# Counters in place of drains, a new order within a slot, and a later first gather in the paged decode of a decoder layer

## Chip, cores and metric

The kernel runs on one core of a Trainium2 chip. The metric is the device time of one execution in microseconds; a run's figure is the median of several executions. The profile is one further execution, recorded instruction by instruction.

## What is computed

One layer of an autoregressive trunk, for one prompt of 1024 tokens and for 8 samples with 8 new tokens each, all in float32. An RMS norm and a wide projection feed three branches: sparse attention (compressed, selected and windowed), a gated convolution and a recurrence. They are joined and projected back. The part that the change touches is the attention of the samples over their cached pages and window:

```python
def _nsa_decode(q, k_c, v_c, k_s, v_s, k_w, v_w, pool_ck, pool_cv, pool_sk, pool_sv, win_k, win_v, page_table, w_ck, w_cv, rel_bias):
    ...
    o_c, p_c = _nsa_compressed(q, q_pos, kc, vc, rel_bias)
    ...
    top_i, valid = _select_blocks(p_c, q_pos, n_sel)
    ...
    ks = jnp.where(is_past, pool_sk[phys[..., None], rows, g5], jnp.pad(k_s, pad)[b5, new_rows, g5])
    vs = jnp.where(is_past, pool_sv[phys[..., None], rows, g5], jnp.pad(v_s, pad)[b5, new_rows, g5])
    key_pos = top_i[..., None] * SEL_BLOCK + s_ar
    o_s = _sel_attend(q, q_pos, ks, vs, key_pos, valid, rel_bias)
    ...
    o_w = _window_dense(q, q_pos, kw, vw, k_pos, rel_bias)
    return o_c, o_s, o_w, _last_rows(kw, w_buf), _last_rows(vw, w_buf)
```

The kernel doesn't gather the selected blocks alone: it loads all cached keys and values of a sample, computes all scores and adds a mask.

## The kernel before

The kernel is one hand-ordered program for each engine, joined by counting semaphores. Its stages: projections with the convolution and the recurrence beside them (to about 500 us), the attention of the prompt tile by tile (`pe_pairs`, to about 671 us), the decode (`pe_decode`, to about 802 us), and the output projection (to the end). TensorE (PE) does matmuls and transposes, VectorE (DVE) and ScalarE (ACT) read PSUM, GpSimd (POOL) issues the indirect gathers and does the last sums of the prompt's attention, SyncE (SP) issues plain loads.

**Decode rounds.** The 8 samples are done in 4 pairs. A round works on two pairs at once: keys and scores of pair `r`, and probabilities and values of pair `p = r - 1`; so there are five rounds (rnd 0 to 4), the first with keys alone, the last with values alone. The cached tokens of a pair are 8 chunks of 512 (c = 0 to 7) and a ninth, the window (`NC` = 8). A round has five slots, `SLOTS = [(0, 1), (2, 3), (4, 5), (6, 7), (NC,)]`. In slot d PE does, in this order:

1. `turn(p, 2d)` and `turn(p, 2d + 1)` (L2025): transposes of the probabilities into the PSUM banks `TURNED`;
2. `pe_decode_keys_turn(pe, r2, chunks[0])` and then `chunks[1]` (L1983): transposes of the keys of the next slot's chunks, 8 for a chunk, into the two banks `KEYS`; both chunks use the same two banks, so the second waits until the first is copied out;
3. `scores(r, mine)` (L2012) of this slot's chunks, into the banks `SCORED`;
4. `values(p, c)` (L2048) of both chunks; in slot 0 `blocks(p)` (L2037), in slot 4 `new_values` (L2061) around the window's values.

**Who copies.** ACT copies turned keys (L1836) and the even turned probabilities (L1824), and does the exponentials `exp` (L1845). An odd chunk is "swapped": one half of its keys is copied by ACT and the other by DVE, in `keys` (L1942, one copy of 64 x 1024). DVE also copies the odd probabilities (L1824), adds masks and finds maxima of the scores in `peak` (L1887, L1890), and in the first slot of rounds 2 to 4 joins the result of the pair before the last (`finish`, L1914 to L1926). DVE's order in a slot: odd probabilities, `finish`, odd keys, peaks.

**Buffers and gathers.** A gather (L1743 for keys, L1755 for values) fetches half of the chunks of one sample; two of them, one for each sample of the pair, make a half (h = 0 for chunks 0 to 3, 1 for chunks 4 to 7), 2 x 1 MB. There is one buffer of keys, so the keys of pair 1 can only be gathered when PE has turned those of pair 0. Before, PE tells this by `pe.drain().then_inc(...)` on four counters: `kused` and `wkused` for keys and window keys (L1986, L1988), `vused` and `wvused` for values (L2052, L2054), and a fifth, `o_d` (L2065), tells DVE that the result of a pair is whole. That is 7 drains in a full round. The last transposes or matmuls of each chunk also count on `kt_ps` or `dv` themselves.

**Around the start of the decode.** `pool_pairs` does the prompt's last joins: for each part a sum (L1577) and, at a tile's end, a product (L1581) that counts on `oz`. At its last part it waits for `kused` and issues the first gathers of pair 1 (`pool_keys(pool, 1, 0)`, L1570) ahead of the last sum. Then `pool_decode` goes on with the second half of the keys, both value halves, and so on in a fixed order. The three last side steps of the prompt's attention (`TAIL_SIDES`: one product with the compressed values, L1595, and two transposes of weights, L1599) are spread over slots 0 to 2 of round 0, each with a DVE step (L1439, L1442). DVE, ACT and POOL may not go on with probabilities before `oz` has reached 8, since the tiles share storage.

**Output.** In round 4 PE fills its gaps with the first products of the output projection (L2171) and then runs it alone.

Of the kernel before, what the change touches and what calls it, by code (L numbers as in the profile page):

```python
# [23 lines left out]
P = 128  # L24
# [8 lines left out]
HD = 64  # L33
# [144 lines left out]
def program(nc, dram, outs, scratch):  # L178
    with ExitStack() as ctx:
# [743 lines left out]
        def carve(a, n):  # L923
# [62 lines left out]
            kt_ps kt_act kt_dve q_swapped dpair kused vused wkused wvused sd_ps sn_ps sd_used mx_sel mx_win ex_d dp_ps o_d o_sb ot_ps   # L986
# [575 lines left out]
        def pool_pairs(pool):  # L1562
            pool.wait_ge(SEM["za_silu"], 2)
            pool_wide(pool, 0)
            for n, m in enumerate(WEIGHTS):
# [3 lines left out]
                if n == len(WEIGHTS) - 1:  # L1569
                    pool.wait_ge(SEM["kused"], 1)  # L1570
                    pool_keys(pool, 1, 0)
# [125 lines left out]

        def after(r, d):

            return (r, SLOTS[d + 1]) if d + 1 < len(SLOTS) else (r + 1, SLOTS[0])  # L1700
# [18 lines left out]
        def keys_bank(b2):  # L1719
            return bank(KEYS + b2)  # L1720
# [52 lines left out]
        def pool_decode(pool):  # L1773
            def keys(pr, h):
                pool.wait_ge(SEM["kused"], 2 * (pr - 1) + h + 1)
                pool_keys(pool, pr, h)

            def values(pr, h):
                before = pr - 1 if h else pr - 2
                if before >= 0:  # L1780
                    pool.wait_ge(SEM["vused"], 2 * before + h + 1)
                pool_values(pool, pr, h)
            keys(1, 1)
            pool.wait_ge(SEM["oz"], NT)
# [11 lines left out]
        def sp_decode(sp):  # L1796
# [6 lines left out]
            for rnd in range(4):  # L1803
                if rnd < 3:
                    sp.wait_ge(SEM["wkused"], rnd + 1)
                    window(rnd + 1, "win_k", kw_d, kw_ld)
                if rnd == 3:

                    for h in range(2):
                        sp.wait_ge(SEM["kused"], 7 + h)  # L1810
                        for k in (2 * h, 4 + 2 * h):
                            sp.dma_start(wo[:, k:k + 2, :], dram["w_out"][:, k:k + 2, :]).then_inc(ld_wo[h], 16)
                if rnd >= 1:
                    sp.wait_ge(SEM["wvused"], rnd)
# [11 lines left out]
        def act_decode(act):  # L1826
            def keys(r, c):
                k = k_no(r, c)
                for b2 in range(2):
# [3 lines left out]
                    o, i = ktc[:, k % 4, b2, :], keys_bank(b2)  # L1833
# [15 lines left out]
            for rnd in range(ROUNDS):  # L1849
                r, p = rnd, rnd - 1  # L1850
                for d in range(len(SLOTS)):
                    if p == 0 and d == 0:
                        act.wait_ge(SEM["oz"], NT)
                    if p >= 0:
                        turned(act, p, 2 * d)
                    r2, chunks = after(r, d)
                    if r2 < 4:
                        keys(r2, chunks[0])
                    if p >= 0 and d < NC // 2:
                        exp(p, 2 + d)  # L1860
                    if r < 4 and d == NC // 2:
                        exp(r, 0)
                        exp(r, 1)
                    if r2 < 4 and len(chunks) > 1:
                        keys(r2, chunks[1])

        def dve_decode(dve):
# [42 lines left out]
            def finish(p):  # L1910
# [9 lines left out]
                dve.wait_ge(SEM["o_d"], p + 1)  # L1920
# [16 lines left out]
            def keys(r, c):  # L1937
# [4 lines left out]
                dve.tensor_copy(ktc[HD:2 * HD, k % 4].rearrange("p b n -> p (b n)"), bank(KEYS, 2)[0:HD]).then_inc(SEM["kt_dve"], 1)  # L1942
# [29 lines left out]
        def pe_decode_keys_turn(pe, r, c):  # L1972
            if c in (0, NC // 2, NC):
                pe.wait_ge(kw_ld if c == NC else kd_ld[c // (NC // 2)], 32 * r + 32)
            k = k_no(r, c)
            for b2 in range(2):
                src = kd[:, b2, c * 512:(c + 1) * 512] if c < NC else kw_d[:, b2, :]
                if k >= 1:
                    pe.wait_ge(SEM["kt_act"], 2 * k - 1 + b2)
                    if b2 == 0:  # L1980
                        pe.wait_ge(SEM["kt_dve"], swapped_to(r, c - 1)) if swapped_to(r, c - 1) else None
                for j in range(4):
                    last = pe.transpose(keys_bank(b2)[:, j * P:(j + 1) * P], src[:, j * P:(j + 1) * P], ident)  # L1983
                last.then_inc(SEM["kt_ps"], 1)
            if c in (NC // 2 - 1, NC - 1):
                pe.drain().then_inc(SEM["kused"], 1)  # L1986
            if c == NC:
                pe.drain().then_inc(SEM["wkused"], 1)  # L1988

        def pe_decode(pe):  # L1990
# [48 lines left out]
            def values(p, c):  # L2039
# [31 lines left out]
            rest = list(TAIL_SIDES)  # L2071
            pe_decode_keys_turn(pe, 0, 1)
            for rnd in range(ROUNDS):
                r, p = rnd, rnd - 1
                for d, mine in enumerate(SLOTS):
                    r2, chunks = after(r, d)
                    if p >= 0:
# [4 lines left out]
                    if r2 < 4:  # L2082
# [435 lines left out]
```

## Time and profile before

| | us |
|---|---|
| median of 3 runs | 924.86 (924.19 to 928.08) |
| the profiled execution | 920.5 |
| its span, first to last instruction | 918.4 |
| PE busy | 866.4 (94%) |
| DVE busy | 621.0 (68%) |
| ACT busy | 369.5 (40%) |
| POOL busy | 121.3 (13%) |
| DMA, over the span | 118.31 MB, mean 129 GB/s |

Busy time is summed for each engine. PE's ends are modelled from the size of an instruction, so successive groups can overlap by some 0.1 us. In the rows below, a time in brackets is the time in which the engine stood idle just ahead of the group, with what ended it; "issue" means that the profile shows nothing that it waited for. L-numbers are lines of the kernel before.

### The profile page before, as it was taken

What the parts mean: (1) busy time and instruction counts of PE and PEld (TensorE: products, weight loads), DVE (VectorE), ACT (ScalarE), POOL (GpSimd) and SP (SyncE); (2) the same over time, 40 slices, a digit from 0 to 9 for tenths busy, and PEclk for the clock granted to TensorE, in tenths of its full rate; (3) what the DMA queues carried; (4) which work ended last, traced back from release to release, by engine and by line L of the source; (5) the groups of instructions that cost most, each with busy time, mean ns of one, the idle gap of its engine ahead of it and who ended that gap; (6) DMA issues with size and microseconds to landing.
All of it is one profiled execution on the core that took longest, in us unless ns stands there. A gap on an engine that the chain in (4) does not pass through costs nothing.

```text
span 918.4 us, 15568 instructions
## 1 busy us (share of the span) xinstructions
PE 866.4 (94%) x5973; PEld 551.1 (60%) x5973; DVE 621.0 (68%) x1149; ACT 369.5 (40%) x878; POOL 121.3 (13%) x129
## 2 busy tenths in 40 slices
PE   6999999999999999999899999998888888999997
PEld 4656665666666666767676776775555655544443
DVE  4688779999888988998466557667875556321222
ACT  4311252310021201025787887776656555410111
POOL 1011210000001011110103222232253220000000
PEclk9999999999999999999999999999999999999999
DMA  8444561422144166440930200000039985522211
GB/s 303 176 138 143 200 206 48 60 53 68 47 137 175 29 223 240 162 161 0 323 166 1 92 3 1 2 1 1 1 109 412 378 336 214 183 94 81 80 61 43
DMA packets 32109, 118.31 MB, mean 129 GB/s; under 512 B 3433, under 2 KB 11771, under 8 KB 22971
## 3 DMA queue, kind: packets, MB, share of 16 engines
q0 software_dynamic: 9360, 68.16, 20.0%
q1 hardware_dynamic: 19053, 43.39, 13.8%
q10 hardware_dynamic: 3623, 5.76, 3.0%
q8 instruction: 48, 0.79, 0.4%
q14 instruction: 25, 0.20, 0.1%
HBM read 108.33 MB, written 13.29 MB: 132 GB/s over the span
## 4 chain that ended last, share of the span: by engine, by line
PE 77%; DVE 10%; ACT 4%; DVEq 3%; issue 3%; DMA 2%; POOL 0%; ACTq 0%; POOLq 0%
PE PS L836 28%; PE PS L2171 12%; PE PS L1616 6%; PE PS L1626 6%; PE PS L1644 5%; PE PS L812 3%; PE PS L1983 3%; DVE main L609 3%; ACT main L1417 2%; PE PS L2025 2%; PE PS L2048 2%; PE PS L2012 2%; DVE main L606 2%; PE PS L1599 1%; DVEq L607 1%
## 5 line engine op out<-in xcount | busy, mean ns | idle before, releaser
L836 PE MATMUL PS<-main 128*128 128x352 f32 (+1 forms) x1056 | 330.1, 472 | 0.0
L836 PEld LDWEIGHTS PS<-main 128*128 128x128 f32 x1056 | 201.3, 191 | 120.7 <-issue 3.6
L1417 ACT ACTIVATE main<-PS,main 128x512 f32<-128x512 f32 (+3 forms) x192 | 103.8, 562 | 50.3 <-DVE main L1457 25.2
L2171 PE MATMUL PS<-main 128*128 128x512 f32 x256 | 111.6, 593 | 0.1
L437 ACT ACTIVATE main<-PS 128x384 f32<-128x384 f32 x24 | 11.8, 490 | 205.5 <-PE PS L836 199.1
L1626 PE MATMUL PS<-cst,main 128*128 128x128 f32 x528 | 73.6, 282 | 15.0 <-ACT main L1417 12.4
L647 DVE SCALAR_TENSOR_TENSOR main<-main,par 128x1022 f32<-128x1022 f32 (+16 forms) x66 | 83.8, 1270 | 5.3 <-issue 0.4
L2171 PEld LDWEIGHTS PS<-main 128*128 128x128 f32 x256 | 47.9, 190 | 58.3 <-issue 58.3
L606 DVE TENSOR_TENSOR main<-main 128x1024 f32<-128x1024 f32 x64 | 75.5, 1220 | 9.6 <-DMA main<-in_cmp_k_dram,row 6.0
L609 DVE TENSOR_TENSOR main<-main 128x1024 f32<-128x1024 f32 (+2 forms) x96 | 75.0, 781 | 7.2
L1626 PEld LDWEIGHTS PS<-cst,main 128*128 128x128 f32 x528 | 57.5, 142 | 30.4 <-ACT main L1417 22.9
L1407 ACT ACTIVATE main<-PS 128x512 f32<-128x512 f32 (+1 forms) x138 | 69.7, 603 | 2.8 <-PE PS L1626 2.4
L1616 PE MATMUL PS<-main 64*128 64x512 f32 (+3 forms) x384 | 68.5, 487 | 0.1
L1644 PE MATMUL PS<-main 128*64 128x128 f32 (+2 forms) x924 | 66.6, 292 | 0.0
L1644 PEld LDWEIGHTS PS<-main 128*64 128x64 f32 x924 | 50.8, 137 | 24.6 <-issue 22.4
L1457 DVE CUSTOM_DVE_ANT_1 PS<-PS,diag 128x512 f32<-128x512 f32 x70 | 46.8, 727 | 16.5 <-PE PS L1616 16.5
L374 POOL DMA_INDIRECT main<-in_cmp_k_dram,row x16 | 19.1, 1192 | 248.7 <-DVE half L611 228.6
L1836 ACT ACTIVATE main<-PS 128x512 f32<-128x512 f32 (+1 forms) x72 | 39.2, 595 | 19.9 <-PE PS L1983 19.5
L2199 ACT ACTIVATE main<-PS 128x512 f32<-128x512 f32 x17 | 10.2, 597 | 89.6 <-PE PS L2171 83.6
L1616 PEld LDWEIGHTS PS<-main 64*128 64x128 f32 x384 | 31.0, 190 | 19.2 <-issue 13.4
L1983 PE MATMUL PS<-cst,main 128*128 128x128 f32 x256 | 35.7, 284 | 7.1 <-ACT main L1836 3.0
L1417 ACT ACTIVATION_READ_ACCUMULATOR main<-PS,main 128x1 f32 x192 | 40.7, 212 | 0.0
(320 smaller groups left out, 1006.5 us busy)
## 6 DMA issues: line engine op xcount, KB each, us to landing
main<-in_w_tiles_dram SPq DMA_DIRECT2D x24, 512.0 KB, 3.7
out_dram<-main SPq DMA_DIRECT2D x18, 256.0 KB, 2.1
main<-in_x_prompt_dram SPq DMA_DIRECT2D x8, 512.0 KB, 9.2
main<-in_w_out_dram SPq DMA_DIRECT2D x4, 1024.0 KB, 7.0
main<-in_x_prompt_dram SPq DMA_DIRECT2D x16, 256.0 KB, 2.9
out_dram<-main SPq DMA_DIRECT2D x4, 512.0 KB, 3.8
diag<-in_win_k_dram SPq DMA_DIRECT2D x8, 256.0 KB, 5.1
diag<-in_win_v_dram SPq DMA_DIRECT2D x8, 256.0 KB
```

The source lines that it names most:

```text
L606: dve.tensor_tensor(rows, rows, w[:, 16 * h:16 * h + 16, :], ALU.mult)
L609: dve.tensor_tensor(stage[:, h, 0:m], stage[:, h, 0:m], stage[:, h, m:2 * m], ALU.add)
L647: dve.scalar_tensor_tensor(full[:, lag:], src[:, 0:T - lag], w(k), full[:, lag:], ALU.mult, ALU.add)
L836: last = pe.matmul(bank(3 * s + j)[:, 0:w], ring[:, s, k * P:(k + 1) * P], xT[:, k, t0:t0 + w], start=(k == 0), stop=(k == KD - 1))
L1407: act.activation(probt[:, k % 2, g, 0:n], turn_set(k, g)[:, 0:n], ACT.Copy).then_inc(SEM["t_sb"], 1)
L1417: last = act.activation(prob[:, k % 2, g, h * nk_ * P:(h + 1) * nk_ * P], score_set(k, g)[:, h * nk_ * P:(h + 1) * nk_ * P], ACT.Exp, scal ...
L1457: dve.tensor_tensor_reduce(v, v, diag[:, 0:h + 1:h, :], 1.0, BIG, ALU.add, ALU.min, m).then_inc(SEM["s_max"], 1)
L1616: last = pe.matmul(score_set(k, g)[:, h * nk_ * P:(h + 1) * nk_ * P], proj[rows, QT + r0 + h, i * P:(i + 1) * P], proj[rows, (KS, KW)[br], ...
L1626: last = pe.transpose(turn_set(k, g)[:, e * P:(e + 1) * P], prob[:, k % 2, g, e * P:(e + 1) * P], ident)
L1644: last = pe.matmul(o, nat[:, br, k0 + e, g * HD:(g + 1) * HD], p, start=(e == 0), stop=(e == nk_ - 1))
L1983: last = pe.transpose(keys_bank(b2)[:, j * P:(j + 1) * P], src[:, j * P:(j + 1) * P], ident)
L2171: last = pe.matmul(out_bank(m, h), proj[:, MIX[k], n * P:(n + 1) * P], wo[:, k, h * 512:(h + 1) * 512], start=(x == 0), stop=(x == KD - 1))
```

## The change

Five edits, all in the decode and at its edge:

1. **Counts for drains.** The counters `kused`, `wkused`, `vused`, `wvused` and `o_d` and their 28 drains go. Who waited for them waits for `kt_ps` or `dv`, which the last transposes and matmuls raise themselves (`keys_used`, `values_used`).
2. **Even keys first.** In each slot PE turns the keys of `chunks[0]` ahead of the probabilities, and those of `chunks[1]` after them. ACT copies in the same order; its exponentials of a new pair (`exp(r, 0)`, `exp(r, 1)`) come behind the odd keys. DVE's order stays.
3. **Two pairs of banks in round 0.** No probabilities are turned there, so odd chunks of round 0 go into `TURNED` and even ones into `KEYS`, and a chunk waits for the copy of the chunk before the last.
4. **Side steps.** The first two of the three side steps stand around the keys of chunk 1, ahead of round 0; the third is in slot 0, behind the even keys.
5. **First gathers.** `pool_keys(pool, 1, 0)` leaves `pool_pairs` and stands in `pool_decode` behind the wait for `oz`; and the order there becomes keys(1,0), values(0,1), keys(1,1), values(1,0), where it was keys(1,0), keys(1,1), values(0,1), values(1,0).

```diff
@@ pool_pairs
                 if n == 4:
                     pool_first_values(pool)
-                if n == len(WEIGHTS) - 1:
-                    pool.wait_ge(SEM["kused"], 1)
-                    pool_keys(pool, 1, 0)
                 if m != LAST_SIDE[i]:
                     pool_wide(pool, n + 1)
@@ helpers
+        def keys_used(eng, r, c):
+
+            eng.wait_ge(SEM["kt_ps"], 2 * (k_no(r, c) + 1))
+
+        def values_used(eng, p, c):
+
+            eng.wait_ge(dv[c % 2], p_par(p, c) + 1)
+
...
-        def keys_bank(b2):
-            return bank(KEYS + b2)
+        def keys_bank(r, c, b2, n=1):
+
+            return bank((TURNED if r == 0 and swapped(c) else KEYS) + b2, n)
+
+        def keys_before(r, c):
+
+            if r == 0:
+                return (r, c - 2) if c >= 2 else None
+            return (r, c - 1) if c else (r - 1, NC)
@@ pool_decode
             def keys(pr, h):
-                pool.wait_ge(SEM["kused"], 2 * (pr - 1) + h + 1)
+                keys_used(pool, pr - 1, 4 * h + 3)
                 pool_keys(pool, pr, h)
...
                 if before >= 0:
-                    pool.wait_ge(SEM["vused"], 2 * before + h + 1)
+                    values_used(pool, before, 4 * h + 3)
                 pool_values(pool, pr, h)
-            keys(1, 1)
             pool.wait_ge(SEM["oz"], NT)
             for stored in nat_out:
                 pool.wait_ge(stored, 64)
+            keys(1, 0)
             values(0, 1)
+            keys(1, 1)
             values(1, 0)
@@ act_decode
                 for d in range(len(SLOTS)):
+                    r2, chunks = after(r, d)
+                    if r2 < 4:
+                        keys(r2, chunks[0])
                     if p == 0 and d == 0:
                         act.wait_ge(SEM["oz"], NT)
                     if p >= 0:
                         turned(act, p, 2 * d)
-                    r2, chunks = after(r, d)
-                    if r2 < 4:
-                        keys(r2, chunks[0])
                     if p >= 0 and d < NC // 2:
                         exp(p, 2 + d)
+                    if r2 < 4 and len(chunks) > 1:
+                        keys(r2, chunks[1])
                     if r < 4 and d == NC // 2:
                         exp(r, 0)
                         exp(r, 1)
-                    if r2 < 4 and len(chunks) > 1:
-                        keys(r2, chunks[1])
@@ dve_decode
             dve.memset(sd[:, NEW + DS:NEW_W], 0.0)
+            dve_side(dve, rest.pop(0))
             keys(0, 1)
+            dve_side(dve, rest.pop(0))
@@ pe_decode_keys_turn
-            k = k_no(r, c)
+            before = keys_before(r, c)
             for b2 in range(2):
                 src = kd[:, b2, c * 512:(c + 1) * 512] if c < NC else kw_d[:, b2, :]
-                if k >= 1:
-                    pe.wait_ge(SEM["kt_act"], 2 * k - 1 + b2)
-                    if b2 == 0:
-                        pe.wait_ge(SEM["kt_dve"], swapped_to(r, c - 1)) if swapped_to(r, c - 1) else None
+                if before is not None:
+                    pe.wait_ge(SEM["kt_act"], 2 * k_no(*before) + b2 + 1)
+                    if b2 == 0 and swapped(before[1]):
+                        pe.wait_ge(SEM["kt_dve"], swapped_to(*before))
...
-            if c in (NC // 2 - 1, NC - 1):
-                pe.drain().then_inc(SEM["kused"], 1)
-            if c == NC:
-                pe.drain().then_inc(SEM["wkused"], 1)
@@ values
                     last.then_inc(dv[c % 2], 1)
-                if c in (NC // 2 - 1, NC - 1):
-                    pe.drain().then_inc(SEM["vused"], 1)
-                if c == NC:
-                    pe.drain().then_inc(SEM["wvused"], 1)
@@ new_values
                     last.then_inc(dv[c % 2], 1)
-                    pe.drain().then_inc(SEM["o_d"], 1)
@@ pe_decode
             rest = list(TAIL_SIDES)
+            pe_side(pe, rest.pop(0))
             pe_decode_keys_turn(pe, 0, 1)
+            pe_side(pe, rest.pop(0))
             for rnd in range(ROUNDS):
                 r, p = rnd, rnd - 1
                 for d, mine in enumerate(SLOTS):
                     r2, chunks = after(r, d)
+                    if r2 < 4:
+                        pe_decode_keys_turn(pe, r2, chunks[0])
                     if p >= 0:
                         turn(p, 2 * d)
                         turn(p, 2 * d + 1)
                     if d == 1 and p >= 1:
                         result(p - 1)
-                    if r2 < 4:
-                        pe_decode_keys_turn(pe, r2, chunks[0])
```

## Rows read from the trace of the kernel before

**Rows 1.** Busy us (and instructions) of each engine, PE's granted clock, DMA share, GB/s.

```profile
700.00:720.00 20.00, 16.98 (x397) 12.02 (x400) 11.25 (x26) 11.61 (x23) 5.61 (x6) 1.00 1.01 420
740.00:760.00 20.00, 16.14 (x302) 11.25 (x310) 10.75 (x32) 12.34 (x26) 3.90 (x5) 1.00 0.93 363
820.00:840.00 20.00, 20.00 (x48) 8.87 (x47) 5.24 (x12) 2.47 (x8) 0.00 (x0) 1.00 0.18 61
```

**Rows 2.** Timeline of PE, round 2, slots 0 and 1: start, length in us, idle before.

```profile
726.19 1.07 PE L2025 MATMUL PS<-cst,main 128*128 128x128 f32 x8 [0.28 <-issue]
...
728.38 1.15 PE L1983 MATMUL PS<-cst,main 128*128 128x128 f32 x8 [0.25 <-ACT main L1836]
729.78 1.09 PE L2012 MATMUL PS<-main,kcn 64*32 64x512 f32 x16 [0.26 <-issue]
...
732.11 1.09 PE L2025 MATMUL PS<-cst,main 128*128 128x128 f32 x8
...
733.15 1.04 PE L1983 MATMUL PS<-cst,main 128*128 128x128 f32 x8
734.43 1.15 PE L1983 MATMUL PS<-cst,main 128*128 128x128 f32 x8 [0.25 <-ACT main L1836]
735.51 1.09 PE L2012 MATMUL PS<-main,kcn 64*32 64x512 f32 x16
```

**Rows 3.** The same timeline, ends of value groups in rounds 2 and 4.

```profile
755.52 0.31 PE L2061 MATMUL PS<-cwb,main 16*32 16x64 f32 x8
756.11 1.06 PE L2025 MATMUL PS<-cst,main 128*128 128x128 f32 x8 [0.28 <-issue]
...
786.04 1.08 PE L2048 MATMUL PS<-main 128*32 128x64 f32 x64
787.05 1.09 PE L2025 MATMUL PS<-cst,main 128*128 128x128 f32 x8
...
789.90 1.10 PE L2048 MATMUL PS<-main 128*32 128x64 f32 x64
791.29 1.06 PE L2025 MATMUL PS<-cst,main 128*128 128x128 f32 x8 [0.29 <-issue]
```

**Rows 4.** The same timeline, the two longest idle stretches of rounds 1 and 2.

```profile
717.99 0.23 PE L1997 MATMUL PS<-main,kcn 64*32 64x16 f32 x2 [1.66 <-issue]
...
747.39 0.38 PE L1983 MATMUL PS<-cst,diag 128*128 128x128 f32 x2 [1.92 <-issue]
```

**Rows 5.** Timeline of POOL at the end of the prompt's attention.

```profile
682.67 1.00 POOL L1743 DMA_INDIRECT main<-in_sel_k_dram,row  x1 [0.16 <-POOL main L1577]
...
684.93 1.30 POOL L1577 TENSOR_TENSOR main<-main 128x512 f32<-128x512 f32 x1
686.30 1.28 POOL L1581 TENSOR_TENSOR main<-main 128x512 f32<-128x512 f32 x1
```

**Rows 6.** Timeline of DVE around round 0: last results of the prompt, last side step.

```profile
670.99 1.46 DVE L1479 COPY main<-PS 128x512 f32<-128x512 f32 x2
...
684.13 0.68 DVE L1442 TENSOR_TENSOR main<-main,PS 128x512 f32<-128x512 f32 x1
```

**Rows 7.** Timeline of PE: end of round 0, wait for pair 1's keys, round 1's slot 1.

```profile
688.40 1.09 PE L2012 MATMUL PS<-main,kcn 64*32 64x512 f32 x16 [0.41 <-DVE sm L1890]
691.69 1.09 PE L1983 MATMUL PS<-cst,main 128*128 128x128 f32 x8 [2.19 <-DMA main<-in_sel_k_dram,row]
...
702.52 1.09 PE L2025 MATMUL PS<-cst,main 128*128 128x128 f32 x8
```

**Rows 8.** DMA view, gather of keys issued at 689.01: count, us to landing.

```profile
main<-in_sel_k_dram,row POOLq DMA_INDIRECT x1, 10.1
```

**Rows 9.** As in group 1, of the stretch behind the wait for pair 1's keys.

```profile
692.80:696.10 3.30, 3.07 (x16) 1.77 (x16) 1.07 (x1) 3.14 (x8) 1.81 (x2) 0.51 1.03 427
```

**Rows 10.** Timeline of DVE, round 2, slot 0: turned probabilities, odd keys.

```profile
727.30 0.69 DVE L1824 COPY main<-PS 128x512 f32<-128x512 f32 x1 [1.29 <-PE PS L2025]
...
729.80 1.22 DVE L1942 COPY main<-PS 64x1024 f32<-64x1024 f32 x1 [0.20 <-issue]
```

More of the change, by code:

```diff
@@ L985, in program @@
             s_ps s_max p_sb t_ps t_sb pv_ps side_ps side_sb o_sb2 stat_gap stat_exp w_ready w_wide mixing oz
-            kt_ps kt_act kt_dve q_swapped dpair kused vused wkused wvused sd_ps sn_ps sd_used mx_sel mx_win ex_d dp_ps o_d o_sb ot_ps
+            kt_ps kt_act kt_dve q_swapped dpair sd_ps sn_ps sd_used mx_sel mx_win ex_d dp_ps o_sb ot_ps
             ld_gp y_ps y_sq y_ms y_rt y_gain y_fold y_out""".split()
@@ L1804, in sp_decode @@
                 if rnd < 3:
-                    sp.wait_ge(SEM["wkused"], rnd + 1)
+                    keys_used(sp, rnd, NC)
                     window(rnd + 1, "win_k", kw_d, kw_ld)
@@ L1809, in sp_decode @@
                     for h in range(2):
-                        sp.wait_ge(SEM["kused"], 7 + h)
+                        keys_used(sp, 3, 4 * h + 3)
                         for k in (2 * h, 4 + 2 * h):
@@ L1813, in sp_decode @@
                 if rnd >= 1:
-                    sp.wait_ge(SEM["wvused"], rnd)
+                    values_used(sp, rnd - 1, NC)
                     window(rnd, "win_v", vw_d, vw_ld)
@@ L1832, in keys @@
                         act.wait_ge(SEM["sd_ps"], k - 3)
-                    o, i = ktc[:, k % 4, b2, :], keys_bank(b2)
+                    o, i = ktc[:, k % 4, b2, :], keys_bank(r, c, b2)
                     if swapped(c):
@@ L1919, in finish @@
                 dve.drain()
-                dve.wait_ge(SEM["o_d"], p + 1)
+                values_used(dve, p, NC + 1)
                 dve.tensor_scalar(osb1, window, sm[:, 45:46], None, ALU.mult)
@@ L1941, in keys @@
                     dve.wait_ge(SEM["sd_ps"], k - 3)
-                dve.tensor_copy(ktc[HD:2 * HD, k % 4].rearrange("p b n -> p (b n)"), bank(KEYS, 2)[0:HD]).then_inc(SEM["kt_dve"], 1)
+                dve.tensor_copy(ktc[HD:2 * HD, k % 4].rearrange("p b n -> p (b n)"), keys_bank(r, c, 0, 2)[0:HD]).then_inc(SEM["kt_dve"], 1)
             rest = list(TAIL_SIDES)
             dve.memset(sd[:, NEW + DS:NEW_W], 0.0)
+            dve_side(dve, rest.pop(0))
             keys(0, 1)
+            dve_side(dve, rest.pop(0))
             for rnd in range(ROUNDS):
@@ L1974, in pe_decode_keys_turn @@
                 pe.wait_ge(kw_ld if c == NC else kd_ld[c // (NC // 2)], 32 * r + 32)
-            k = k_no(r, c)
+            before = keys_before(r, c)
             for b2 in range(2):
                 src = kd[:, b2, c * 512:(c + 1) * 512] if c < NC else kw_d[:, b2, :]
-                if k >= 1:
-                    pe.wait_ge(SEM["kt_act"], 2 * k - 1 + b2)
-                    if b2 == 0:
-                        pe.wait_ge(SEM["kt_dve"], swapped_to(r, c - 1)) if swapped_to(r, c - 1) else None
+                if before is not None:
+                    pe.wait_ge(SEM["kt_act"], 2 * k_no(*before) + b2 + 1)
+                    if b2 == 0 and swapped(before[1]):
+                        pe.wait_ge(SEM["kt_dve"], swapped_to(*before))
                 for j in range(4):
-                    last = pe.transpose(keys_bank(b2)[:, j * P:(j + 1) * P], src[:, j * P:(j + 1) * P], ident)
+                    last = pe.transpose(keys_bank(r, c, b2)[:, j * P:(j + 1) * P], src[:, j * P:(j + 1) * P], ident)
                 last.then_inc(SEM["kt_ps"], 1)
-            if c in (NC // 2 - 1, NC - 1):
-                pe.drain().then_inc(SEM["kused"], 1)
-            if c == NC:
-                pe.drain().then_inc(SEM["wkused"], 1)
         def pe_decode(pe):
@@ L2132, in sp_output @@
             sp.dma_start(gpost, dram["g_post"].to_broadcast([P, D])).then_inc(SEM["ld_gp"], 16)
-            sp.wait_ge(SEM["vused"], 8)
+            values_used(sp, 3, NC - 1)
             for m in range(3):
@@ L2192, in act_output @@
         def act_output(act):
-            act.wait_ge(SEM["vused"], 8)
+            values_used(act, 3, NC - 1)
             for m, n in enumerate(OUT):
```

## The prediction

> **What bounds the kernel now.** I read the table of windows first. TensorE is busy for 20.00 us of 20 in the output projection, but for 16 to 17 us of 20 in the decode rounds [rows 1]. ACT and DVE are busy for some 11 to 12 us of 20 there, so neither is full: PE loses 3 to 4 us of every 20 to waits of its own. Behind the decode PE runs without a gap to the end, so what the decode saves moves the end by as much, as long as the output's loads keep pace; they are triggered by PE's own progress, so they move along. The DMA engines are the second thing to look at: their share is 1.01 at 420 GB/s in 700 to 720 and 0.93 in 740 to 760 [rows 1]. In round 1 the gathers are at the rate limit, later there is some room.
>
> Then the timeline of PE in one round. It shows three kinds of gap. (a) Ahead of the second chunk of keys 0.25 us, until ACT has copied the first out of the same banks [rows 2]. (b) 0.26 to 0.29 us with the releaser "issue" exactly where the code has a drain [rows 2, 3]. (c) One stretch of 1.66 and 1.92 us in a round, also "issue" [rows 4]. Last, the start: PE waits 2.19 us for pair 1's keys at 691.69 [rows 7], and behind that the granted clock is 0.51, its lower level of 1.2 GHz, for 3.3 us [rows 9].
>
> **Drains.** With a drain between keys and scores, the scores start 1.40 us after the keys (728.38 to 729.78); without, 1.08 us (734.43 to 735.51) [rows 2]: 0.32 us each. Between values and the next slot's first transposes it is 1.39 us with (789.90 to 791.29) and 1.01 us without (786.04 to 787.05): 0.37 us [rows 3]. The drain behind the last new values: 0.59 us from 755.52 to 756.11 for a group of 0.31 us [rows 3], so some 0.3. For the two others (`wkused`, `wvused`) I take 0.2 and 0.3, between nothing and 0.37. A full round then holds 2 x 0.32 + 2 x 0.37 + 0.3 + 0.2 + 0.3 = 2.2 us. I count only what lies behind slot 1 of round 1, because up to there the gathers set the pace (below): round 1 without its first key drain 1.9, rounds 2 and 3 2.2 each, round 4 (values alone) 1.35. **Sum 7.6 us saved.** The waits that replace them cost nothing: POOL and SP, who wait for the counters, only get them earlier.
>
> **Even keys first.** Two chunks of keys and the step to the scores take 2.36 us (733.15 to 735.51) [rows 2]. A group of 8 transposes costs 0.93 us where nothing holds it (its 1.04 us include a tail that overlaps), so 1.86 us would do: 0.5 us for each slot that turns two chunks. With the probabilities between the two chunks, ACT has 0.93 us more to empty the banks. Behind slot 0 of round 1 there are 3 + 4 + 3 such slots: **5.0 us saved.**
>
> What is late next? The even keys of a slot now follow the values of the slot before and need its odd keys copied, by ACT and by DVE. A slot without gaps is 3 x 0.93 + 1.02 + 1.03 = 4.84 us. In it the odd keys are turned by 2.90 us, and DVE's copy of 1.22 us [rows 10] ends at 4.15 us, 0.55 us ahead of need with the 0.14 us to PE. ACT is busy for 12.34 us of 20 [rows 1], that is for some 3.6 us of a slot of 5.9, and fits too. So a normal slot holds. But in slot 0 of rounds 2 and 3 DVE does `finish` between its copy of probabilities and its odd keys: from 727.30 to 729.80 is 2.50 us [rows 10]. The probabilities are now turned 0.93 us later, so the copy of the keys starts at 2.06 + 2.50 = 4.56 us into the slot and PE can go on at 5.92, where it could at 5.10 (today's 5.92 from 726.19 to 732.11 [rows 2] less 0.5 and 0.32). In the order of before, a whole group of transposes stood between. **Cost 2 x 0.8 = 1.6 us.**
>
> **The start.** POOL's last join before: the gather issues at 682.67 and 683.98, then a sum of 1.30 and a product of 1.28 us, which ends at 687.6 [rows 5], behind DVE's last side step at 684.81 [rows 6]. Now DVE's copies of the last parts end at 672.45 [rows 6], the first side step follows (1.0 us on PE, 0.7 on DVE), then keys 1 with DVE's copy, the second and the third side step on both: DVE is done at about 677.9. POOL's two sums and product take 1.3 us each: `oz` is full at about 680.7. The first gather leaves there, 1.9 us earlier than at 682.67, although it now stands behind the join. The keys it overwrites have been turned by 678. The other waits in its path are for stores from long before.
>
> Round 0 itself gains little: PE must first wait for DVE (0.9 us ahead of the first side step), later DVE, with the odd keys and the peaks of two chunks in each slot, sets the pace. I get the last scores of two chunks at 687.3 instead of 688.40 [rows 7]. Pair 1's first keys land at 689.8 instead of 691.6, so PE waits 1.4 us.
>
> **The queue behind it.** Values(0,1), two gathers and 2.1 MB, are now ahead of keys(1,1), and all gathers go through one queue. Before, the second gather of keys(1,1) landed 10.1 us after 689.01 [rows 8], at 699.1. With 2.1 MB more ahead at 420 GB/s [rows 1] that is 5.0 us later, less 1.9 us for the earlier start: 702.2. PE needs these keys first thing in slot 1 of round 1, and would get there at about 699, so it waits some 3 us, where before it waited for nothing. Slot 1 began at 702.52 [rows 7]: **0.3 us saved**, not 3. Behind that the queue is not late any more: pair 2's first keys, by the same count, land near 712 and are needed at 718.
>
> A wait of that length can lower the clock. Before, the lower level came behind some 4 us in which PE did little, with a wait of 2.19 us at the end [rows 7, 9]; behind the 1.92 us wait amid full work [rows 4] the clock stayed up. I take it that it falls once, behind slot 1, and that 3.3 us at the lower level cost 1.6 us. The drop of before lay ahead of slot 1, where the gathers hide it now. **Cost 1.6 us**, between 0 and 1.6.
>
> **The long stretches stay.** The 1.66 and 1.92 us "issue" gaps come 29.1 us apart, about one round, but not at a drain: one falls inside a group of 8 transposes [rows 4]. At that point the DMA engines are full. They look like the loading of PE's own code, one such wait in a fixed number of instructions, and the change removes only a few of those. The Trainium skill, page "Runtime: NRT & Kernel Launch", section "Instruction fetch mechanics", says that an engine's instructions are streamed in 16 KiB blocks by its own DMA queue and that crossing a block's boundary is mostly hidden. The trace disagrees here: up to 1.92 us show. By the page's "hidden" these gaps would have another cause and might go with the drains, which would be 4 us more saved; since they fall between plain transposes I don't count on it.
>
> **Sum.** -0.3 - 7.6 - 5.0 + 1.6 + 1.6 = -9.7 us. On the profiled execution: 920.5 - 9.7 = 910.8. The median of before is 4.4 us above its profiled execution; I expect the same offset, so 924.86 - 9.7 = **915.2 us**.
>
> **Rivals.**
> - *The queue does no harm* (keys(1,1) land by 700, or the clock stays up). For it: the landing before trailed its bytes by about 2 us, which may shrink. Against: full engines from 684 on. Gain 1.6 + 1.7 more: 912.
> - *The drains' gaps are the wait for something else*, a copy or an exponential, and half of the term stays, or the counts don't do what they should. Against: slots without a drain show no gap in the same places [rows 2]. 924.86 - 5.9 = 919.
> - *The gather leaves late.* The join does not move forward (the side steps wait for DVE), and the gather leaves at 687.6, where `oz` was full before: 4.9 us later than before. Then keys(1,1) land 6.8 us later than in my count, at 709.0. Total -9.7 + 6.8 = -2.9: 922.
> - *DVE's odd copy gates every slot* (slower than before). It is the new loop: copy, even keys, probabilities, odd keys, copy. Its slack is 0.55 us. Every us beyond that is paid in each of the 10 slots. It eats the gain from 0.55 + 0.97 = 1.5 us of delay on, and makes the kernel slower by 0.5% from 2.0 us on, as if every slot had a `finish` in it: 930. Against: DVE stood idle for 1.29 us ahead of its copy of probabilities even in the slot with a `finish` [rows 10].
>
> **Chances.** Forecast (913 to 918) 0.50, no harm from the queue 0.20, half the drains 0.13, late gather 0.10, DVE gates 0.04, else 0.03. The range leaves out the last two and the outer half of the late gather: 910.5 to 921. A measurement of this kernel tells about 0.5% (4.6 us) from no change. Faster by more than that (under 920.2): 0.86. Within: 0.10. Slower: 0.04.
>
> **What would show it.** Drains: no "issue" gaps of 0.26 to 0.29 in PE's rows, and keys to scores 1.08 us everywhere. Order: no 0.25 us ahead of the odd keys, normal slots of 4.8 to 5.0 us; in slot 0 of rounds 2 and 3 a wait of about 0.8 us for L1942's successor on DVE, ahead of the even keys of slot 1. Start: first gather near 680.7, a wait of 1 to 2 us for pair 1's first keys and a new one of 2 to 4 us for the second half of them. I am wrong if the first gather leaves after 684, if normal slots stay above 5.4 us, or if the new wait is absent.

## Result and the profile after

| | before | after |
|---|---|---|
| median, us | 926.25 (4 runs, 924.19 to 928.08) | 915.12 (4 runs, 913.32 to 918.36) |
| profiled execution, us | 920.5 | 914.66 |
| span, us | 918.4 | 912.6 |
| instructions | 15568 | 15526 |

Ratio of the runs 0.9892, 95% interval 0.9854 to 0.9929. A second measurement of the same kernel, in another set of runs, gave 0.9897 (0.9873 to 0.9921). The change makes the kernel 1.0 to 1.2% faster, 9.5 us by the second ratio and 11.1 us by the difference of the medians; forecast were 9.7 us and 915.2 us.

The two profiled executions differ by less, 5.8 us. Where, the timeline of PE shows. Three rows of before first: a third long stretch without a visible wait, in round 3 (the forecast showed those of rounds 1 and 2, [rows 4]), the start of round 4, and the first products of the output behind the decode:

```profile
775.87 0.38 PE L2025 MATMUL PS<-cst,main 128*128 128x128 f32 x2 [0.94 <-issue]
...
783.19 1.06 PE L2025 MATMUL PS<-cst,main 128*128 128x128 f32 x8 [0.28 <-issue]
...
802.32 5.41 PE L2171 MATMUL PS<-main 128*128 128x512 f32 x12
```

And of after (L1998 are key transposes, L2036 probabilities, L2023 scores, L2059 values, L2179 the output):

```profile
690.07 1.48 PE L2023 MATMUL PS<-main,kcn 64*32 64x512 f32 x16 [2.77 <-issue]
...
703.48 1.09 PE L1998 MATMUL PS<-cst,main 128*128 128x128 f32 x8
...
705.28 1.04 PE L1998 MATMUL PS<-cst,main 128*128 128x128 f32 x8
706.25 1.09 PE L2023 MATMUL PS<-main,kcn 64*32 64x512 f32 x16
707.27 1.10 PE L2059 MATMUL PS<-main 128*32 128x64 f32 x64
708.30 1.09 PE L1998 MATMUL PS<-cst,main 128*128 128x128 f32 x8
...
723.84 1.09 PE L1998 MATMUL PS<-cst,main 128*128 128x128 f32 x8
...
728.99 0.32 PE L2059 MATMUL PS<-main 128*32 128x64 f32 x3 [0.45 <-issue]
729.72 0.80 PE L2059 MATMUL PS<-main 128*32 128x64 f32 x38 [0.41 <-issue]
...
737.18 0.49 PE L1998 MATMUL PS<-cst,main 128*128 128x128 f32 x3 [1.04 <-issue]
...
752.97 1.09 PE L1998 MATMUL PS<-cst,main 128*128 128x128 f32 x8
...
759.24 0.52 PE L2059 MATMUL PS<-main 128*32 128x64 f32 x18 [1.50 <-issue]
...
777.33 1.09 PE L2036 MATMUL PS<-cst,main 128*128 128x128 f32 x8
...
796.53 5.42 PE L2179 MATMUL PS<-main 128*128 128x512 f32 x12
```

Each full slot now begins with the even keys (L1998). Slot by slot, with [rows 2, 3, 7] for before:

| stretch | before | after | difference | forecast |
|---|---|---|---|---|
| up to slot 1 of round 1 | 702.52 | 703.48 | +1.0 | -0.3 |
| its slots 1 to 4 | 23.67 | 20.36 | -3.3 | -3.4 |
| round 2 | 29.92 | 29.13 | -0.8 | -3.4 |
| round 3 | 27.08 | 24.36 | -2.7 | -2.9 |
| round 4 | 19.13 | 19.20 | +0.1 | -1.35 |
| lower clock behind slot 1 | | | 0 | +1.6 |
| sum | | | -5.8 | -9.7 |

So a total that fits hides terms that don't. What went as said: keys to scores takes 0.97 us (705.28 to 706.25), where it was 1.40 with a drain and 1.08 without [rows 2], and values to the next slot 1.03 us (707.27 to 708.30) against 1.39 [rows 3]. The 0.25 us ahead of the odd keys are gone. What did not: there is no wait for keys(1,1) at 703.48; instead PE stood for 2.77 us ahead of the last scores of round 0; and in rounds 1 to 4 there are idle stretches of 0.4 to 1.5 us, all with the releaser "issue" (those of round 1, at 702.02, 702.75, 713.89 and 714.63, are of 0.4 to 0.5 us). The windows (busy time of PE, PEld, DVE, ACT, POOL, then PE's granted clock, DMA share, GB/s) answer [rows 1, 9]:

```profile
690.00:693.40 3.40, 3.33 (x24) 1.75 (x24) 0.26 (x4) 0.25 (x1) 1.59 (x2) 0.60 1.01 413
700.00:720.00 20.00, 18.04 (x407) 12.91 (x392) 11.73 (x29) 11.38 (x24) 6.02 (x7) 1.00 1.00 404
740.00:760.00 20.00, 17.00 (x370) 12.00 (x362) 12.36 (x36) 11.25 (x23) 3.43 (x4) 1.00 0.98 369
684.00:729.00 45.00, 38.38 (x654) 26.30 (x652) 26.49 (x74) 28.61 (x56) 14.60 (x16) 0.96 1.00 401
```

The DMA share in 740 to 760 has risen from 0.93 to 0.98; over 684 to 729 it is 1.00. The lower clock (0.60 in 690 to 693.4) still lies ahead of slot 1. GpSimd's first gather left at 681.19, where it was 682.67 [rows 5] and 680.7 was forecast; 683.73 is the first of values(0,1), 687.23 the first of keys(1,1):

```profile
681.19 1.00 POOL L1755 DMA_INDIRECT main<-in_sel_k_dram,row  x1 [0.27 <-POOL main L1578]
...
683.73 0.94 POOL L1767 DMA_INDIRECT main<-in_sel_v_dram,row  x1 [0.30 <-issue]
...
687.23 0.94 POOL L1755 DMA_INDIRECT main<-in_sel_k_dram,row  x1 [1.32 <-PE PS L1998]
```

### The profile page after: what moved, and what is told of

Its sections match the earlier page's. It is cut to its first block, busy times and chain, and to the rows that moved or that the text cites. A ratio compares the mean times of both kernels' runs of the same rounds, so it can differ in the third digit from the quotient of the medians.

```text
span 912.6 us, 15526 instructions
## 1 busy us (share of the span) xinstructions
PE 864.1 (95%) x5973; PEld 551.8 (60%) x5973; DVE 620.5 (68%) x1149; ACT 368.1 (40%) x878; POOL 121.2 (13%) x129
## 4 chain that ended last, share of the span: by engine, by line
PE 78%; DVE 11%; ACT 3%; DVEq 3%; issue 3%; DMA 1%; another core or an unknown queue 0%; ACTq 0%; POOL 0%; POOLq 0%
PE PS L836 28%; PE PS L2179 12%; PE PS L1613 6%; PE PS L1623 6%; PE PS L1641 5%; PE PS L812 3%; PE PS L1998 3%; DVE main L609 3%; PE PS L2059 2%; ACT main L1417 2%; PE PS L2036 2%; PE PS L2023 2%; DVE main L606 2%; PE PS L1596 1%; DVEq L607 1%
## 5 line engine op out<-in xcount | busy, mean ns | idle before, releaser
L2179 PE MATMUL PS<-main 128*128 128x512 f32 x256 | 111.6, 593 | 0.0
L2179 PEld LDWEIGHTS PS<-main 128*128 128x128 f32 x256 | 47.9, 190 | 58.1 <-issue 58.0
L1998 PE MATMUL PS<-cst,main 128*128 128x128 f32 x256 | 35.0, 281 | 2.4 <-issue 1.0
```

Source lines behind the costliest of these rows:

```text
L1998: last = pe.transpose(keys_bank(r, c, b2)[:, j * P:(j + 1) * P], src[:, j * P:(j + 1) * P], ident)
L2179: last = pe.matmul(out_bank(m, h), proj[:, MIX[k], n * P:(n + 1) * P], wo[:, k, h * 512:(h + 1) * 512], start=(x == 0), stop=(x == KD - 1))
```

## Experiments

All ratios are to the kernel before in the same set of runs, with 95% intervals. There are three sets: the first has `a1` to `a4` (median of before 919.25 us), the second `after_again`, `b1_counts_only`, `b2_thin` and `c1_finish_later` (924.5), the third the others (921.06). A ratio of 0.0011 is 1 us. An interval is some 2 to 3 us wide to each side, so two ratios that are less than about 0.003 apart are not told apart. Where a run is set beside the kernel after, that is at 0.9897, from the second set.

**The drains, from both sides.** In `a1_drains_back` the kernel after gets its drains back:

```diff
                 last.then_inc(SEM["kt_ps"], 1)
+            if c in (NC // 2 - 1, NC - 1, NC):
+                pe.drain()
...
                     last.then_inc(dv[c % 2], 1)
+                if c in (NC // 2 - 1, NC - 1, NC):
+                    pe.drain()
...
                 if k == 1:
                     last.then_inc(dv[c % 2], 1)
+                    pe.drain()
```

> The kernel after, with its 28 drains put back as bare drains; the counts stay. If a drain costs what the rows of before say (0.3 to 0.37 us each, 7.6 us behind slot 1 of round 1), this kernel is 6 to 8 us slower than the kernel after, about 922. If, as the trace after suggests, much of that gain was given back in longer idle stretches without a visible wait (released by 'issue'), such stretches shrink here and it is only 2 to 4 us slower, 917 to 919. If the drains cost nothing, 915.

Measured 0.9994 (0.9973 to 1.0015): all of the gain is gone. In its trace PE waits for keys(1,1) at the start of slot 1 of round 1, as forecast for the kernel after:

```profile
704.40 1.09 PE L1998 MATMUL PS<-cst,main 128*128 128x128 f32 x8 [3.06 <-DMA main<-in_sel_k_dram,row]
```

`b1_counts_only` is the kernel before with edit 1 alone, that is with `keys_used` and `values_used` for the five counters and without the drains.

```diff
-                pool.wait_ge(SEM["kused"], 2 * (pr - 1) + h + 1)
+                keys_used(pool, pr - 1, 4 * h + 3)
...
-            if c in (NC // 2 - 1, NC - 1):
-                pe.drain().then_inc(SEM["kused"], 1)
```

> The kernel before with edit 1 alone: counts for the 28 drains. Putting the drains back into the kernel after cost 1.0% of the time (9.4 us), so if the edits add up this one is 7 to 9 us faster than before, ratio 0.990 to 0.992. Theory: PE is the bound of the rounds and every drain is paid. Rival: in the old order the freed time goes to the waits for the copies (ACT ahead of the second keys) and for pair 1's keys; then only 3 to 5 us, ratio 0.995 to 0.997.

Measured 0.9912 (0.9890 to 0.9933), 8.2 us. The drains are worth 8 to 9 us from either side (8.9 by putting them back, give or take 3); the forecast had 7.6.

**The order.** `a2_old_order` is the kernel after with edit 2 undone, on PE and ACT:

```diff
-                    if r2 < 4:
-                        pe_decode_keys_turn(pe, r2, chunks[0])
                     if p >= 0:
                         turn(p, 2 * d)
                         turn(p, 2 * d + 1)
                     if d == 1 and p >= 1:
                         result(p - 1)
+                    if r2 < 4:
+                        pe_decode_keys_turn(pe, r2, chunks[0])
```

> The kernel after with edit 2 undone: PE turns probabilities first, then both chunks of keys, and ACT copies in the old order. The two banks pairs of round 0 and the counts stay. If the order saves 0.5 us a slot in 10 slots, less 1.6 us lost to DVE's join: 3 to 5 us slower than after, about 919. If the gain goes where 'issue' gaps grow: within 1.5 us of it, 916. The 0.25 us waits for ACT ahead of the odd keys must be back.

Measured 0.9940 (0.9919 to 0.9962), 4 us slower than after, give or take 3; forecast for the order net of DVE's join: 3.4 us. The 0.25 us waits for ACT are back, and here too the wait for keys(1,1) shows:

```profile
701.88 3.52 PE L1998 MATMUL PS<-cst,main 128*128 128x128 f32 x16 [2.06 <-DMA main<-in_sel_k_dram,row]
```

But `d1_counts_order`, the kernel before with edits 1 and 2 and without 3 to 5, says that the order alone adds nothing:

```diff
+                    if r2 < 4:
+                        pe_decode_keys_turn(pe, r2, chunks[0])
                     if p >= 0:
                         turn(p, 2 * d)
                         turn(p, 2 * d + 1)
...
-                    if r2 < 4:
-                        pe_decode_keys_turn(pe, r2, chunks[0])
```

> The kernel before with edits 1 and 2 (counts, even keys first) and without 3, 4 and 5 (banks of round 0, side steps, first gathers). Counts alone gave 0.9912; undoing the order in the kernel after cost 0.0048. If edits 3 to 5 gain nothing or lose a little, this kernel is at 0.986 to 0.989. If the earlier first gather (1.5 to 3.3 us earlier in the traces) is paid, it is at 0.991 to 0.993.

Measured 0.9932 (0.9905 to 0.9959), against 0.9912 for the counts alone: no gain that could be told. The first branch of my expectation (0.986 to 0.989) was missed; the result lies beside the second, by which the earlier first gather is paid. The order and edits 3 to 5 pay only together (0.9897), by some 3 us for edits 3 to 5 and 4 for the order, at the edge of what the intervals tell. The traces say where, not why: slot 1 of round 1 begins at 702.26 here and at 698.74 in `a3_keys_together`, which has all five edits but the new place of keys(1,1), and from there to the output both take 94 us (93.74 and 94.09). And PE's long stretches without a visible wait (0.5 us and more, from slot 1 on) add up to 7.7 us here, to 4.5 in before and to 1.3 in `b1_counts_only`, which has short ones besides (last section).

**The gathers' queue.** `a3_keys_together` gathers keys(1,1) ahead of values(0,1) again:

```diff
             keys(1, 0)
-            values(0, 1)
             keys(1, 1)
+            values(0, 1)
             values(1, 0)
```

> The kernel after with keys(1,1) gathered directly behind keys(1,0), ahead of values(0,1), all behind oz. My prediction had the new order of the gathers cost some 3 us of waiting in slot 1 of round 1. The trace after shows no wait there, so this theory now expects no change (within 1.5 us of the kernel after). The rival, that the late keys still hold the start back through something else, expects 2 to 3 us faster, 912.

Measured 0.9892 (0.9862 to 0.9922): as after. Yet its trace has slot 1 of round 1 at 698.74, without a wait, 4.7 us earlier than the trace of after:

```profile
697.66 1.13 PE L2059 MATMUL PS<-main 128*32 128x64 f32 x64
698.74 1.08 PE L1998 MATMUL PS<-cst,main 128*128 128x128 f32 x8
...
725.77 0.43 PE L2059 MATMUL PS<-main 128*32 128x64 f32 x15 [1.38 <-issue]
...
734.15 0.49 PE L1998 MATMUL PS<-cst,main 128*128 128x128 f32 x3 [2.33 <-issue]
...
762.26 0.82 PE L1998 MATMUL PS<-cst,main 128*128 128x128 f32 x6 [1.73 <-issue]
```

`b3_gather_early` leaves the new order of the queue but issues keys(1,0) ahead of the prompt's last join, as before the change:

```diff
+                if n == len(WEIGHTS) - 1:
+                    keys_used(pool, 0, 3)
+                    pool_keys(pool, 1, 0)
                 if m != LAST_SIDE[i]:
                     pool_wide(pool, n + 1)
...
-            keys(1, 0)
             values(0, 1)
             keys(1, 1)
```

> The kernel after with the first gathers of pair 1 back ahead of the prompt's last join on GpSimd. They leave at about 678.3 instead of 680.8 us, the join and with it the values' gathers 2.5 us later. If the start is set by pair 1's first keys, 1 to 2 us faster than after (0.988); if by keys(1,1) behind them in the queue or by DVE's peaks in round 0, no change (0.9897).

Measured 0.9875 (0.9841 to 0.9909): 2 us faster than after if anything, not told apart. Its trace shows the forecast's queue in full: a wait of 2.86 us for keys(1,1), then transposes that take 1.68 us for 8 instead of 1.04, at a clock of 0.66 over 5 us:

```profile
701.55 1.09 PE L2000 MATMUL PS<-cst,main 128*128 128x128 f32 x8 [2.86 <-DMA main<-in_sel_k_dram,row]
702.48 1.68 PE L2038 MATMUL PS<-cst,main 128*128 128x128 f32 x8
```

```profile
701.50:706.50 5.00, 4.95 (x40) 4.14 (x40) 1.29 (x2) 4.00 (x7) 0.00 (x0) 0.66 1.00 416
```

So both mechanisms of the forecast's start exist, wait and clock. What they cost at the end is not shown. In the traces `a3_keys_together` begins slot 1 2.8 us ahead of `b3_gather_early` and ends 1.7 us ahead (spans of 908.9 and 910.6 us); the ratios point the other way, by less than they can tell.

**Where the rest goes: thinned gathers.** `a4_thin` and `b2_thin` are the kernels after and before, in which all gathers of the selected keys and values but those of pair 0 and the first values of pair 1 fetch a quarter; what pairs 1 to 3 read besides is left out. Instructions, waits and the number of gathers stay.

```diff
-                pool.indirect_dma_start(kd[:, b2, h * 2048:(h + 1) * 2048], None, half_rows("sel_k"),
+                w = 2048 if pr == 0 else 512
+                pool.indirect_dma_start(kd[:, b2, h * 2048:h * 2048 + w], None, half_rows("sel_k", 4096 // w),
```

> The kernel after with the gathers thinned: all gathers of the selected keys and values but those of pair 0 and the first values of pair 1 fetch 512 instead of 2048 columns, so the cached keys and values of pairs 1 to 3 are mostly wrong in this kernel; the number and place of the gathers, the waits and all engine work are the same. Theory: PE's 'issue' gaps in the decode (some 8 us in rounds 1 to 4 and 2.8 us at the end of round 0) come from full DMA engines; they go, the decode is 8 to 11 us shorter, 904 to 907, and no step to the lower clock. Rival (the gaps belong to the instruction stream or to the mere issue of a gather): the gaps stay at the same places and lengths and the time stays at 913 to 915.

> The kernel before with the same thinned gathers as a4_thin (the cached keys and values of pairs 1 to 3 are mostly wrong in it). Its distance to a4_thin (0.9787) is the change's gain with the DMA engines out of the way. By the sum of my prediction without the terms of the gathers (drains 7.6 plus about 0.3 in slot 0, order 5.0 plus 0.5, less 1.6 for DVE's join, and the earlier start 1.3 to 2 us) that is 13 to 14 us, so this kernel is at ratio 0.993 to 0.994. If code loading in a full queue costs the kernel before as much as the one after (9 us), it is at 0.989.

Measured: after 0.9787 (0.9758 to 0.9816), before 0.9957 (0.9942 to 0.9972). With the DMA engines out of the way the change is worth 0.0170, 15.7 us (13 to 14 were expected); with full gathers 9.5. Full DMA engines cost the kernel before 4 us and the kernel after 10 us: some 6 us of the change's gain are given back to them. The intervals leave 2 to 10 us for this, and the two thinned kernels were measured in different sets, so only their ratios may be compared. Within one set `a3_keys_together`, as fast as after, is 0.0105 (9.7 us) above `a4_thin`. The trace of `a4_thin` shows the decode as the forecast had it, at a DMA share of 0.61 instead of 1.00:

```profile
684.00:729.00 45.00, 42.36 (x815) 30.89 (x814) 32.16 (x88) 32.71 (x66) 15.98 (x18) 1.00 0.61 207
```

```profile
717.32 1.04 PE L2038 MATMUL PS<-cst,main 128*128 128x128 f32 x8
...
722.33 1.06 PE L2000 MATMUL PS<-cst,main 128*128 128x128 f32 x8 [0.90 <-DVE main L1957]
723.23 1.04 PE L2038 MATMUL PS<-cst,main 128*128 128x128 f32 x8
...
728.16 1.04 PE L2038 MATMUL PS<-cst,main 128*128 128x128 f32 x8
```

A normal slot is 4.93 us (723.23 to 728.16; forecast 4.84, or 4.8 to 5.0). The slot with DVE's join is 5.91 us (717.32 to 723.23; forecast 5.92), with 0.90 us of idle time ahead of the even keys (722.33) for DVE's copy of the odd ones. And the long "issue" stretches are gone, but for one of 0.5 us.

**What the long stretches are.** `b4_shift` puts 128 bare drains at the start of PE's program, so that all later instructions lie 128 places further on:

```diff
+            for _ in range(128):
+                pe.drain()
             pe_startup(pe)
```

> The kernel after with 128 bare drains at the start of PE's program, where PE waits for its first loads anyway. They move every later instruction of PE by half a block of 256. If the idle stretches of 1.0 to 2.6 us without a visible wait are the loading of PE's code, they stand 64 matmuls earlier (their last matmul before is number 4493, 4868, 4993 where it was 4557, 4932, 5057) and the time stays within 2 us of after. If they belong to the work (a bank, a wait), they stay at the same matmuls.

Counting PE's matmuls from the start of the program, the single "issue" stretches of 0.5 to 1.5 us stand at numbers 4557, 4681, 4932, 5307 and 5432 in the trace of after, and at these or at others of the same series (4181, 4432, 4807, 5057), with up to 2.3 us, in all traces with PE's program of after and full gathers; their distances are 125 or multiples of it, within 1. In `b4_shift` the long ones stand at 4245, 4745 and 5245, halfway between those of the series, and none at its numbers:

```profile
720.99 0.42 PE L2059 MATMUL PS<-main 128*32 128x64 f32 x12 [1.72 <-issue]
...
749.01 0.43 PE L2059 MATMUL PS<-main 128*32 128x64 f32 x15 [1.81 <-issue]
...
774.89 0.50 PE L2059 MATMUL PS<-main 128*32 128x64 f32 x18 [1.31 <-issue]
```

They move with the place in the program, not with the work: in after the one at 737.18 is in a group of keys, here all three are among values. The DMA engines' own records say what is waited for. Among their packets are some of 16 KB and of the kind "instruction" on a queue q8. One of them is moved at 735.00 to 735.95 in the trace of after, and PE goes on at 737.18 (window 735 to 736: packets, MB, share):

```profile
q8 instruction: 1, 0.02, 6.0%
```

So it is with each of the single stretches of 0.5 us and more from slot 1 of round 1 on, in the traces of before, of after and of all experiments: each ends 1.2 to 1.6 us behind the end of such a packet, also in `b4_shift`. So this is the loading of PE's code, in blocks of which one holds 125 matmuls with their weight loads. (That q8 carries PE's code and not another engine's is read from this timing.) The packets are not slower in full engines, they are late: the one ahead of number 4557 takes 0.9 to 1.1 us in `a4_thin`, in after and in `a3_keys_together`, but it begins when PE is at number 4446, 4534 and 4556. With thinned gathers a single stretch of 0.5 us is left (number 5307). I expected the numbers 64 lower; half a step of 125 up or down is the same. The time was 0.9922 (0.9895 to 0.9950), 2.3 us above after where at most 2 were expected: the drains at the start were not free, PE's first matmul came at 9.94 instead of 7.31 us.

`after_again` is the kernel after itself.

> The changed kernel itself, once more, on the chip of the runs beside it. Expected ratio to before 0.989 to 0.990. Its trace shows whether the idle stretches released by 'issue' (2.8 us at the end of round 0, pairs of 0.4 us among the values, single ones of 1.0 and 1.5 us) stand at the same instructions as in the first trace. If they are a property of the program they do; if they come from code loading that races the gathers, their places and lengths differ by execution.

Measured 0.9897. The single stretches stand at matmuls of the same series with other lengths: the one at number 4557 took 1.04 us in the first trace and 2.33 us here, the one at 4932 1.50 us in both, the one at 4681 is missing here and 5057 has one of 1.17 us:

```profile
689.68 1.47 PE L2023 MATMUL PS<-main,kcn 64*32 64x512 f32 x16 [2.67 <-DVE sm L1903]
...
701.52 0.33 PE L2059 MATMUL PS<-main 128*32 128x64 f32 x4 [0.41 <-issue]
702.27 0.76 PE L2059 MATMUL PS<-main 128*32 128x64 f32 x36 [0.42 <-issue]
...
738.72 0.49 PE L1998 MATMUL PS<-cst,main 128*128 128x128 f32 x3 [2.33 <-issue]
...
760.45 0.52 PE L2059 MATMUL PS<-main 128*32 128x64 f32 x18 [1.50 <-issue]
```

**Tries at a faster kernel.** `c1_finish_later` moves DVE's join behind the odd keys:

```diff
-                    if d == 0 and p >= 1:
-                        finish(p - 1)
...
                         keys(r2, chunks[1])
+                    if d == 0 and p >= 1:
+                        finish(p - 1)
```

> The kernel after with one more move: DVE's join of the pair before the last (finish) stands behind the odd keys instead of ahead of them. By the thinned run the even keys of slot 1 wait 0.6 to 0.9 us for DVE in rounds 2 and 3. If that is paid, this kernel is 1 to 2 us faster than after (ratio about 0.0015 lower). If the gaps of code loading cover it, as in the trace after, no difference.

Measured 0.9869 (0.9847 to 0.9891), beside 0.9897 (0.9873 to 0.9921) in the same set: 2.6 us, not told apart for certain. `c2_finish_keys_together` has this and the order of `a3_keys_together`.

> The kernel after with DVE's join moved behind the odd keys (0.9869 alone against 0.9897) and with keys(1,1) gathered ahead of values(0,1) (0.9892 alone). If both are paid: 0.984 to 0.986, the fastest so far. If the order of the gathers does nothing, as its own run said: 0.987.

Measured 0.9886 (0.9855 to 0.9917), above both values expected: nothing on top. No version was shown to beat the kernel after.

## Why the forecast was right, and where it wasn't

**Drains.** Right in mechanism and size (7.6 forecast, 8.2 alone, about 9 when put back). Reading pairs of like places with and without a drain gave it.

**Even keys first.** Right in mechanism; 3.4 us net forecast, 4 us measured by undoing it, but nothing when added to the counts without edits 3 to 5. The forecast took the terms as additive. They aren't: by the counts the five edits hold 8.2 us from one and 1.3 us from the other four.

**DVE's join.** Right in a clean trace (a slot of 5.91 us against 5.92). In the full kernel it can be covered by another stop at the same place: in after by the short pauses at 728.99 and 729.72 in round 2 and by the loading of code at 759.24 in round 3. In `b4_shift` PE waits 0.90 us for it in round 2.

**The start.** The first gather was forecast at 680.7 and left at 681.19. The wait for keys(1,1) and the lower clock behind it were forecast and are in the traces of `b3_gather_early`; the wait is also in those of `a1_drains_back`, `a2_old_order` and `b4_shift`. In the trace of after PE was late for another reason (2.77 us ahead of the last scores of round 0), so the wait did not show. The forecast set slot 1 at 0.3 us earlier than before; it was 1.0 us later in after, 1.0 us earlier in `b3_gather_early` and 3.8 us earlier in `a3_keys_together`, where the wait is absent. Whether the wait costs the kernel its length at the end is open.

**"The long stretches stay."** This is the step that failed. They were taken as fixed, 1.66 and 1.92 us a round [rows 4], and so stood in the sum at nothing. Their cause was named rightly, but not what follows from it. In before they add up to 4.5 us from slot 1 of round 1 on (three of them); in the traces with edits 1 and 2, full gathers and without the short pauses of the last section, to 9.3 us in `a3_keys_together`, 8.0 in `c2_finish_keys_together`, 7.7 in `d1_counts_order`, 6.0 in `b3_gather_early` and 4.8 in `b4_shift`. By these traces the missed term is 0.3 to 4.8 us, by the thinned runs 6 with 2 to 10 left open. An explanation that fits, but was not tested by itself: PE takes its code at its own pace, so a PE that works faster needs the next block sooner from engines that are no less full. The page "Runtime: NRT & Kernel Launch" of the Trainium skill, section "Instruction fetch mechanics", has instructions streamed in blocks of 256 by a DMA queue of the engine's own, which fits `b4_shift` and the packets of queue q8; that it is mostly hidden holds at a DMA share of 0.61 and not at 1.00.

What made the missed term good can be seen in one trace, that of `a3_keys_together`, which differs from after by the place of keys(1,1) and measured as fast. Its span is 9.5 us shorter than that of before. From slot 1 to the output it gains 5.7 us (94.09 against 99.80), where the forecast had 11.0 without the clock; 4.8 of the 5.3 us between are the longer loading of code. The other 3.8 us are won ahead of slot 1, where the forecast had 0.3, and the 1.6 us booked for the clock were not lost (its clock stays up from there to the output). For after itself this is not shown: its own traces have the short pauses in place of part of the loading. The forecast of 9.7 us was thus right in part by luck, with a term of some us missed and others too dear.

**The rivals.** Late gather, DVE gating every slot and half the drains are refuted by 681.19, by slots of 4.93 us and by `a1_drains_back`. "The queue does no harm" is left open: it was priced at 3.3 us, and after (0.9897) and `a3_keys_together` (0.9892) differ by 0.5 us, give or take 3.5.

## What to carry to other kernels

A drain whose only purpose is to raise a counter cost the engine about a third of a microsecond each time in this kernel; if the last instruction before it can raise the counter itself, use that. Before a saving on a bound engine is added up, look at what it fetches in proportion to its own pace, its code too: where the DMA engines were full here, part of the saving came back as idle time that no wait explains. To find it, count instructions from stop to stop and look for packets of the kind "instruction" just ahead of the restart. To learn how much it is, thin the transfers and leave the instructions.

## What the runs showed beyond that

In the first trace of after and in all four traces of the second set, PE stops twice for 0.4 us among the values of slots 0 and 2 of rounds 1 and 2 (728.99 and 729.72 above, 701.52 and 702.27 in `after_again`): it goes on 2.0 and 2.7 us after GpSimd begins to issue a pair of key gathers, thinned or not. Its share is about 1.6 us each time, over 6 us in all (the 64 matmuls from 700.80 last to 703.48 where 1.03 us is normal), and 1.3 and 5 us in `b2_thin`. In the traces of the other two sets it is absent with the same code. In the sets with it the kernel before took 924.5 and 926.25 us, in those without 919.25 and 921.06; the profiled execution of before (920.5) has none. This would account for why the two first traces differ by 5.8 us and the medians by 11. In those of these traces that have PE's program of after (after, `after_again`, `c1_finish_later`) the counts of PE's last keys of round 0 reach ACT, DVE and GpSimd about 2 us after the matmuls end by the model, which makes the 2.77 us (2.67 in `after_again`). What it is was not found.
